# Two weight panels interleaved by block behind each norm, and the cumulated log decays stacked on 128 partitions

## What is computed

```python
h_lat = rmsnorm(x_lat, norm_w[i, 0]) * (1 + sc_l) + sh_l
h_ctx = rmsnorm(x_ctx, norm_w[i, 0]) * (1 + sc_c) + sh_c
y_lat, y_ctx = hgrn2_mixer(...)  # or mamba2_mixer: h @ w_in, scan, readout @ w_out
x_lat = x_lat + g_l * y_lat
x_lat = x_lat + g2_l * swiglu(rmsnorm(x_lat, norm_w[i, 1]) * (1 + sc2_l) + sh2_l, ...)
# in the Mamba-2 scan, per chunk:
cum = jnp.cumsum(dtc * a.reshape(g, hpg), axis=2)
seg = cum[:, :, :, None] - cum[:, :, None]
lmat = jnp.exp(jnp.where(causal, seg, -jnp.inf))
y_diag = jnp.einsum('bctsgh,bcsghp->bctghp', cb[..., None] * lmat, xdt)
```

## Time and profile before

| | |
|---|---|
| median of 3 runs | 2405.87 us (2405.26 to 2407.23) |
| the profiled execution: its time | 2407.6 us |
| its span in the trace | 2405.9 us |
| TensorE busy | 2183.6 us (91%) |
| VectorE busy | 1078.7 us (45%) |
| ScalarE busy | 836.0 us (35%) |
| mean granted clock of TensorE | 0.941 of full speed |

### The profile page before, as it was taken

How to read it: one execution, slowest core, us unless ns; L and a number is a source line. 1 busy time by engine, 2 the same in 40 slices (tenths; PEclk the granted TensorE clock), 3 DMA queues, 4 the chain that set the end, 5 groups by cost and what they waited for, 6 DMA issues and landing times.

```text
span 2405.9 us, 33890 instructions
## 1 busy us (share of the span) xinstructions
PE 2183.6 (91%) x13300; PEld 1921.9 (80%) x13314; DVE 1078.7 (45%) x1501; ACT 836.0 (35%) x1242; POOL 43.7 (2%) x67
## 2 busy tenths in 40 slices
PE   5899898997879999999998699899997598999997
PEld 3889888886778999999998687777773486888886
DVE  4455455556442222222223757676765434332333
ACT  2343343443223331122221454646362323532322
POOL 1000000000000000000000000000000000000000
PEclk7999999998889999999999799999997598999998
DMA  6322222221314332234222021212110232333331
GB/s 258 112 80 80 71 66 67 80 71 53 114 44 131 113 105 72 76 107 130 91 72 82 18 77 38 62 36 69 35 52 27 87 94 65 98 108 88 97 107 59
DMA packets 296558, 198.00 MB, mean 82 GB/s; under 512 B 4900, under 2 KB 288925, under 8 KB 295837
## 3 DMA queue, kind: packets, MB, share of 16 engines
q1 hardware_dynamic: 293965, 180.03, 24.7%
q0 software_dynamic: 2512, 16.80, 1.8%
HBM read 186.32 MB, written 10.49 MB: 82 GB/s over the span
## 4 chain that ended last, share of the span: by engine, by line
PE 64%; issue 23%; DVE 7%; ACT 2%; DMA 1%; POOL 1%; SPq 0%; DVEq 0%; ACTq 0%; POOLq 0%
PE G L275 51%; PE G L308 2%; PE S L1312 1%; PE S L1163 1%; PE S L547 1%; DVE hn L424 1%; DVE hlo L432 1%; PE S L521 1%; POOL rstd L400 1%; PE S L1159 1%; PE S L1325 1%; PE S L390 1%; ACT whi L254 1%; DVE cum L704 1%; PE G L314 1%
## 5 line engine op out<-in xcount | busy, mean ns | idle before, releaser
L275 PE MATMUL G<-hhi,whi 128*128 128x384 f32 (+1 forms) x2320 | 717.5, 373 | 37.7 <-DVE hlo L432 24.8
L258 DVE TENSOR_TENSOR wlo<-raw,whi 128x1024 fp32r<-128x1024 f32 (+1 forms) x225 | 288.1, 1281 | 921.2 <-ACT whi L254 921.1
L275 PE MATMUL G<-hlo,whi 128*128 128x384 f32 (+1 forms) x2320 | 670.2, 352 | 0.0
L275 PE MATMUL G<-hhi,wlo 128*128 128x384 f32 (+1 forms) x2320 | 669.3, 352 | 0.0
L254 ACT ACTIVATE whi<-raw 128x1024 fp32r<-128x1024 f32 (+1 forms) x225 | 248.8, 1106 | 1005.4 <-PE G L275 506.7
L275 PEld LDWEIGHTS G<-hhi,whi 128*128 128x128 f32 x2320 | 420.6, 192 | 104.5 <-issue 57.5
L275 PEld LDWEIGHTS G<-hhi,wlo 128*128 128x128 f32 x2320 | 431.2, 191 | 20.7
L275 PEld LDWEIGHTS G<-hlo,whi 128*128 128x128 f32 x2320 | 433.3, 192 | 18.0
L275 PE MATMUL G<-mhi,whi 128*128 128x384 f32 (+1 forms) x656 | 208.7, 361 | 14.1 <-DVE mlo L1444 14.1
L275 PE MATMUL G<-mhi,wlo 128*128 128x384 f32 (+1 forms) x656 | 208.3, 361 | 0.0
L275 PE MATMUL G<-mlo,whi 128*128 128x384 f32 (+1 forms) x656 | 208.3, 361 | 0.0
(11 more groups left out here) (247 smaller groups left out, 1945.6 us busy)
## 6 DMA issues: line engine op xcount, KB each, us to landing
raw<-in_ffn_w_in_dram SPq DMA_DIRECT2D x88, 512.0 KB, 3.7
adaw<-in_ada_w_dram SPq DMA_DIRECT2D x40, 1024.0 KB, 5.3
raw<-in_ffn_w_out_dram SPq DMA_DIRECT2D x32, 704.0 KB, 4.5
raw<-in_ssm_w_in_dram SPq DMA_DIRECT2D x41, 512.0 KB, 3.8
raw<-in_hg_w_in_dram SPq DMA_DIRECT2D x40, 512.0 KB, 3.8
ada<-in_ada_w_dram SPq DMA_DIRECT2D x4, 2048.0 KB, 13.1
raw<-in_ssm_w_out_dram SPq DMA_DIRECT2D x16, 512.0 KB, 3.9
raw<-in_hg_w_out_dram SPq DMA_DIRECT2D x8, 512.0 KB, 4.0
```

The source lines that it names most:

```text
L258: dve.tensor_tensor(wlo[pn.slot][:, 0:kt, :], raw[pn.slot][:, 0:kt, :], f32(whi[pn.slot][:, 0:kt, :]), ALU.subtract).then_inc(s["lo"], 1)
L275: ins = pe.matmul(G[:, tl.slot, g0:g0 + n], w[pn.slot][:, k, :], r[:, k_base + k, t0:t0 + n], start=(first and k == 0 and i == 0), stop=(l ...
```

## The change

Two things are changed.

**A pair of panels behind each norm.** `product` is cut into `product_begin`, `product_block` and `product_end`. The new `product_pair` works off panels A and B behind a norm together: A0, A1, B0, A2, B1, and so on to A7, B6, B7. Both panels' weights and both tiles must be ready before A0. The end of A, with the slab's rows, stands between A7 and B6. At the FFNs the first iteration of TensorE's loop is taken out for this (`begin`), and the loop's other iterations no longer carry the waits on `hlo`. At the Mamba-2 layer the pair is the `dt` panel and the first input panel. The loops of the other engines stay as they were.

**High and low decays in one matmul.** `cuhi` and `culo` (64 partitions each) become one tensor `cuts` of 128 partitions, high above low. `sel` becomes 128 rows with the selector repeated, so that one matmul gives high plus low. Its four parts are written with four small DVE copies per group instead of two.

```diff
+        def product_block(pe, pn, tl, rhi, rlo, k, kt, segs, k_base=0, first=True, last=True, turn=None):
+            if turn is not None and k == kt - 1:
+                prev = tl + (-1)
+                pe.wait_ge(took[prev.slot], prev.turn + 1)
+            for i, (w, r) in enumerate(((whi, rhi), (whi, rlo), (wlo, rhi))):
...
+        def product_end(pe, tl, ins, rows=None, turn=None):
             if rows is not None:
                 ins = slab_rows(pe, tl, rows)
             if turn is not None:
                 ins = slab_turn(pe, tl, turn)
             ins.then_inc(s["pan"], 1)
...
+        def product_pair(pe, pn, tl, segs, need, rows=None, turn=None):
+
+            product_begin(pe, pn, tl)
+            product_begin(pe, pn + 1, tl + 1)
+            for k in range(KT + 1):
+                if k < KT:
+                    need(k)
+                    ins = product_block(pe, pn, tl, m["hhi"], m["hlo"], k, KT, segs)
+                if k == KT - 1:
+                    product_end(pe, tl, ins, rows=rows)
+                if k:
+                    ins = product_block(pe, pn + 1, tl + 1, m["hhi"], m["hlo"], k - 1, KT, segs, turn=turn)
+            product_end(pe, tl + 1, ins, turn=turn)
...
-            for j in range(5):
+            if h is None:
+                product_pair(pe, hg, hg, SEGS, h_need(pe, 0), rows=hn_ * 2, turn=m["mrow0"])
+            for j in range(2 if h is None else 0, 5):
...
-                with eng.Fori(0, FH - 1) as i:
+                peel = begin is not None and hf == 0
+                if peel:
+                    begin(pn, tl)
+                with eng.Fori(1 if peel else 0, FH - 1) as i:
...
+            def begin(pn, tl):
+                slab = l == 0
+                product_pair(pe, pn, tl, segs, h_need(pe, 1 + 2 * l), rows=SL_F0 if slab else None,
+                             turn=m["mrow1"] if slab else None)
...
         def dt_tensor(pe):
-            pn = At(PAN_DT)
-            product(pe, pn, pn, m["hhi"], m["hlo"], KT, SEGS, need=h_need(pe, N2))
+
+            assert PAN_SS == PAN_DT + 1
+            product_pair(pe, At(PAN_DT), At(PAN_DT), SEGS, h_need(pe, N2))
...
-                    for d in (0, 1):
-                        ins = dve.tensor_copy(m["sel"][:, d * HPG:(d + 1) * HPG],
-                                              ident[0:2 * NH, bass.ds(q * HPG + d * NH, HPG)])
+                    for part in (0, 2 * NH):
+                        for d in (0, 1):
+                            ins = dve.tensor_copy(m["sel"][part:part + 2 * NH, d * HPG:(d + 1) * HPG],
+                                                  ident[part:part + 2 * NH, bass.ds(q * HPG + (d * NH + part), HPG)])
...
             for d in (0, 1):
-                for part in ("cuhi", "culo"):
-                    pe.matmul(S[:, d, :], m["sel"][:, d * HPG + hh:d * HPG + hh + 1].to_broadcast([2 * NH, P]),
-                              m[part][:, :], start=(part == "cuhi"), stop=False)
+                pe.matmul(S[:, d, :], m["sel"][:, d * HPG + hh:d * HPG + hh + 1].to_broadcast([P, P]),
+                          m["cuts"][:, :], start=True, stop=False)
                 ins = pe.matmul(S[:, d, :], m["identb"][:, :], m[f"neg{d}"][:, :], start=False, stop=True)
```

More of the change, by code:

```diff
@@ L259, in split_lo, with product_begin @@
                               f32(whi[pn.slot][:, 0:kt, :]), ALU.subtract).then_inc(s["lo"], 1)
-        def product(pe, pn, tl, rhi, rlo, kt, segs, k_base=0, first=True, last=True, need=None,
-                    rows=None, turn=None, between=None):
+        def product_begin(pe, pn, tl, first=True):
             pe.wait_ge(s["lo"], pn.n + 1)
@@ L285, in product @@
             ins.then_inc(s["pan"], 1)
+        def product(pe, pn, tl, rhi, rlo, kt, segs, k_base=0, first=True, last=True, need=None,
+                    rows=None, turn=None, between=None):
+            product_begin(pe, pn, tl, first)
+            for k in range(kt):
+                if need is not None:
+                    need(k)
+                ins = product_block(pe, pn, tl, rhi, rlo, k, kt, segs, k_base, first, last, turn)
+                if between is not None:
+                    between(k)
+            product_end(pe, tl, ins, rows, turn)
+        def product_pair(pe, pn, tl, segs, need, rows=None, turn=None):
[3 more added lines that the diff above has]
+                if k < KT:
+                    need(k)
+                    ins = product_block(pe, pn, tl, m["hhi"], m["hlo"], k, KT, segs)
[4 more added lines that the diff above has]
+            product_end(pe, tl + 1, ins, turn=turn)
         def slab_load(sp, a, l, col, before, norms=1):
```

40 lines of the change are left out of this document (16 added, 24 removed).

## The result

| | before | after |
|---|---|---|
| median of the timed runs, us | 2406.18 (2405.26 to 2407.23, 4 runs) | 2385.73 (2383.71 to 2389.12, 4 runs) |
| profiled span, us | 2405.9 | 2382.8 |
| mean granted clock | 0.941 | 0.937 |

The ratio of the medians is 0.9911, 95% interval [0.9896, 0.9926]: 20.5 us gained, where the working had 34.6. The two profiled spans stand 23.1 apart. The median is 13.7 above my 2372 and 0.7 beyond the slow end of the range (2385); on the scale of the 2405.87 that I started from, 0.9911 of it is 2384.5, just inside. The heads with panels beside them gave what was said; 8 us went in the stretches between the heads, and the last group gave 3 less than said.

A forecast was written before the change was run, and what follows sets the result against it. The prediction took TensorE with its clock as the bound. Its terms, 4.5 + 2.6 + 0.8 + 0.3 + 15.5 + 11.7 - 0.8, summed to 34.6 us gained, for a forecast of 2372 us, range 2362 to 2385.

The forecast's parts named there:

- last group: Last Mamba-2 head group, without panels: 1.52 us saved per cold head, 1.03 for one warm head, 11.7 us in all.
- start and first norm: HGRN2 norm: the paired panels let C start at 86.5 to 87.6 instead of 91.96; 4.5 us gained.
- first FFN's norm: Norm of the first FFN: C starts at 740.1 to 741.2 instead of 743.89; 2.6 us gained.
- `dt` norm: Third norm (step sizes): A7 ends near 1340.7 instead of near 1341.5; 0.8 us gained.
- The part on the segments: Warm Mamba-2 head segments: four matmuls on 128 rows replace six, saving 1.03 us per head.
- Rival 1: Head segments: the extra 0.1 us step belongs to the broadcast selector and stays; 2377.6 us, chance 0.24.
- The walk through a group: Three head groups with panels: ACT stops waiting for segments, TensorE stalls near heads 6 and 7; 5.15 us per group, 15.5 total.
- rival 3: Head groups: ACT makes up lost time and TensorE sets the pace; 24.7 us instead of 15.5, 2362, chance 0.09.
- The 24 us of idle time before `dt_turn`: Third norm: `dt_turn` starts hardly earlier against the norm, TensorE's idle time doubled to some 24 us.
- Selector copies: Two more small DVE casts per group, ahead of the first values TensorE waits for; 0.8 us lost.
- Rival 4: Three head groups: TensorE's pauses drop the clock to 0.50 for panels 6 to 9; slower, 2416 us, chance 0.05.
- Rival 2: The norms give nothing, each gain ending at another wait; 26.4 us from the heads, 2379.5, chance 0.12.

The follow-up runs named there:

- before_casts: The kernel before, with its two selector casts cut into four of half the width; 2413.08 us, ratio 1.0015.
- late_casts: The kernel after, with the four selector casts moved behind the group's first chain steps; 2381.84 us, ratio 0.9882 against before.
- pairs_only: The kernel before plus only the interleaved panels behind the four norms, segments still on 64 rows; 2408.3 us over 11 runs, ratio 0.9996.
- filler: The kernel after, with ten matmuls that nobody reads in each group's wait for `wx`; 2375.62 us, ratio 0.9864 against before.
- wx_first: The kernel after, with DVE's first `wx` product ahead of the next panel's split and the four casts; 2368.79 us, ratio 0.984 against before.
- wx_first_layer0: wx_first with pairs kept at the first two norms only; 2371.29 us, ratio 0.984 against before.

## Why the prediction came out as it did

On the scale of the two spans, step by step:

| step | said | measured | |
|---|---|---|---|
| start and first norm | 4.5 | 4.4 | mechanism right; the size has up to 3 us of the clock's luck in it |
| first FFN's norm | 2.6 | 1.4 | 2.3 at C's start, ACT's `mrow` as said; C's first block runs at the lower clock |
| `dt` norm | 0.8 | 0.1 | idle time 11.9 to 17.6, not to 24 |
| heads in three groups | 15.5 | 15.7 | 5.24 per group |
| last group | 11.7 | 8.5 | 1.32 per head instead of 1.52, first head cold |
| casts, and all between the heads | -0.8 | -8.1 | the step that failed |
| last FFN and the rest | 0.3 | 1.0 | |
| sum | 34.6 | 23.1 | |

The part on the segments held to 0.01 us: 1.03 per head said, 1.02 measured. Rival 1, that the 0.1 stays with the selector, is refuted by the row of 0.24. The walk through a group held too: ACT stops waiting, TensorE waits 1.11 before the segment of head 6 and 1.44 before the values of head 7, and 5.24 come out where 5.15 stood. That refutes rival 3. The 24 us of idle time before `dt_turn` were a wrong sum: only the six blocks of B that move ahead of A7 lengthen it, 11.9 + 6 x 1.04 = 18, and the trace has 17.6.

The step that failed is the one on what lies between the heads. I counted only "Selector copies" there: "Two took 0.23 together, so 0.15 to 0.3 more, four times", 0.8 lost. The stretches took 8.1 more. The direct price of the casts is 1.6 (0.39 each time). The rest is clock, 8.2 us more lost, less other small changes: 3.4 at the first group's wait for `wx`, which the casts lengthen, 3.4 behind the values of head 7, whose wait the short segments lengthen, and 1.4 at the ends of the stretches. I asked of an edit ahead of a wait only how much longer the wait gets, and not which granted clock follows. Rival 4 had this mechanism, and one of its places ("before the values of head 7"). I gave it 0.05 because pauses of 0.75 left the clock alone, though my own walk made that pause longer; and its price was wrong the other way, 15 per group for four panels at the lower clock, where one fall costs 1.7. How much of the 8.1 belongs to the casts stays open: `before_casts` turns 0.56 us of longer waits into some 4 us of time, but `late_casts` takes the casts out of the wait and its trace keeps 8.3, and `pairs_only` has 6.7 with every wait as before. The Trainium skill, "TensorE: Matmul & The Clock Gate", section on HAM oscillation, which I cited there, was the right warning: `filler` bears it out, and the traces show falls at waits of 1.4 to 3.2 us, shorter than the 4 us that I had set against it.

Rival 2 (the norms give nothing) was right that the medians show nothing of the pairs alone (0.9996); its 2379.5 was not, since it kept all that was said of the heads. Its reason was wrong too. The pairs gain their microseconds in layer 0, and the scan's clock takes them back; with the long wait gone some 4 appear. In the last group I mis-sized one term: four matmuls at 0.43 and 0.24 of latency are 1.96, the rows show 2.16. And I priced the first head as warm, as it was before, when the clock fell at 1843 behind it. Now it falls at 1824.5, ahead of it: 0.7 lost where 1.0 was to be gained. So the time ended at the edge of the range with two terms well short, and it was the width of the range that held it, not the sum.

What stays open: why the kernels with pairs meet the clock worse in an unchanged scan. Their start of the scan is shifted by 5.5 us against everything before it, and a wait of 2.42 is followed by a fall at 1537.8 in after and by none at the same place before. That fits a dependence on when the wait comes, but no run varied this alone. Nor did a run vary the wait before the values of head 7 alone.

## What to carry to other kernels

A wait of one and a half to three microseconds in a stream of matmuls can have two prices, its length and the clock behind it; count both before an edit lengthens it, also where the edit only makes the work ahead of it quicker, and look first for a producer's instruction that can go ahead of unrelated work. A gain of a few microseconds upstream of such waits may not arrive: measure it again once they are gone. Where a wait can't be removed, cheap matmuls on idle data in it are worth trying.

## What was unexpected of the hardware

- At full load around it, TensorE's clock fell to 0.50 during or just behind a wait of 2.65 us or more for `wx` in 34 of 36 places, at one of 2.1 to 2.4 (the sum of squares) in 30 of 39, behind one of 1.4 (the values of head 7) in 18 of 30, and behind the same one of 0.75 in none of nine. It cost 1.7 us, in some places 3.4.
- Executions of one kernel differ by this: 21 runs of before have spans of 2403.2 us at a mean clock of 0.943 to 2410.2 at 0.939. A difference of 5 us between two profiled executions may be nothing else, as the first norm's C shows (91.96, 89.02 and 90.19 with the same code). So can 7.5 us over the four stretches (`wx_first` and `wx_first_layer0`).
- A change between matmuls on 64 and on 128 rows cost 0.15 us each time; a segment with two halves of 64 rows took 1.95 us, one with 128 rows 0.93.
